# The low part of one weight slab in four, added up by a DMA from SBUF instead of VectorE's subtraction

## The reference

```python
def _even_mixer(h, w_in, a_conv, b_conv, b_conv_bias, b_ln_g, b_ln_b, w_out):
    p = h @ w_in                                   # (512, 2048) @ (2048, 7*1024)
    a_x, a_b, a_c, a_z, b_val, b_gate, b_z = jnp.split(p, 7, axis=-1)
    ya = a_b * _causal_dwconv(a_c * a_x, a_conv)   # 3 taps
    yb = b_val * jax.nn.sigmoid(b_gate)
    yb = _causal_dwconv(yb, b_conv) + b_conv_bias  # 31 taps
    yb = jax.nn.silu(_layernorm(yb, b_ln_g, b_ln_b))
    u = jnp.concatenate([ya * jax.nn.silu(a_z), yb * jax.nn.silu(b_z)], axis=-1)
    return u @ w_out
```

## Time and profile before

| | us |
|---|---|
| time, three runs | 1404.67 median (1404.5 to 1405.18) |
| span of the profiled execution | 1402.8 |
| PE busy | 1377.8 (98%) |
| DVE busy | 698.9 (50%) |
| ACT busy | 384.5 (27%) |
| POOL busy | 109.9 (8%) |
| mean traffic of the DMA engines | 110 GB/s |

### The profile page before, as it was taken

How to read it: one execution, slowest core, us unless ns; L and a number is a source line. 1 busy time by engine, 2 the same in 40 slices (tenths; PEclk the granted TensorE clock), 3 DMA queues, 4 the chain that set the end, 5 groups by cost and what they waited for, 6 DMA issues and landing times.

```text
span 1402.8 us, 16146 instructions
## 1 busy us (share of the span) xinstructions
PE 1377.8 (98%) x6466; PEld 1156.4 (82%) x6466; DVE 698.9 (50%) x767; ACT 384.5 (27%) x413; POOL 109.9 (8%) x101
## 2 busy tenths in 40 slices
PE   5999999999999999999999999999999999999997
PEld 4988888888888888888888899888888888888886
DVE  7588888888753223334332585444522222722333
ACT  5332233222222122223321353222222223512220
POOL 5100000000008200000000000000000003400000
PEclk9999999999999999999999999999999999999999
DMA  8243333434243333333422364333333322262204
GB/s 245 61 111 95 94 112 98 120 90 112 71 127 90 109 90 91 90 105 137 178 90 95 119 205 121 92 99 105 96 90 100 109 90 90 64 236 90 90 30 180
DMA packets 208307, 154.82 MB, mean 110 GB/s; under 512 B 2576, under 2 KB 187024, under 8 KB 205968
## 3 DMA queue, kind: packets, MB, share of 16 engines
q1 hardware_dynamic: 207120, 145.94, 35.1%
q10 hardware_dynamic: 1152, 8.39, 1.6%
HBM read 145.93 MB, written 8.39 MB: 110 GB/s over the span
## 4 chain that ended last, share of the span: by engine, by line
PE 96%; DVE 2%; issue 1%; DMA 0%; ACT 0%; DVEq 0%; POOLq 0%; POOL 0%
PE bank L417 32%; PE bank L418 32%; PE bank L419 32%; DVE h_lo L971 1%; DVE scratch L977 1%; PE bank L447 0%; DVE rows L964 0%; DMA rows<-x_t 0%; DVE diagonals L942 0%; DVE w_lo L986 0%; DVE rows L1128 0%; PE bank L476 0%; PE bank L485 0%; ACT scratch L682 0%; PE bank L545 0%
## 5 line engine op out<-in xcount | busy, mean ns | idle before, releaser
L417 PE MATMUL bank<-h_hi,w_hi 128*128 128x512 f32 (+1 forms) x1600 | 597.3, 373 | 4.9 <-DVE h_lo L971 4.8
L418 PE MATMUL bank<-h_lo,w_hi 128*128 128x512 f32 (+1 forms) x1600 | 595.3, 372 | 0.0
L419 PE MATMUL bank<-h_hi,w_lo 128*128 128x512 f32 (+1 forms) x1600 | 595.3, 372 | 0.0
L909 DVE TENSOR_TENSOR w_lo<-raw,w_hi 128x2048 fp32r<-128x2048 f32 x121 | 280.3, 2317 | 215.7 <-ACT w_hi L650 194.7
L417 PEld LDWEIGHTS bank<-h_hi,w_hi 128*128 128x128 f32 x1600 | 301.4, 188 | 59.3 <-issue 4.5
L419 PEld LDWEIGHTS bank<-h_hi,w_lo 128*128 128x128 f32 x1600 | 301.4, 188 | 52.6
L418 PEld LDWEIGHTS bank<-h_lo,w_hi 128*128 128x128 f32 x1600 | 301.4, 188 | 52.4 <-issue 0.5
L650 ACT ACTIVATE w_hi<-raw 128x2048 fp32r<-128x2048 f32 x122 | 233.3, 1912 | 238.2 <-PE bank L419 189.6
L1004 DVE SCALAR_TENSOR_TENSOR rows<-shifted,vecs,rows 128x512 f32 x256 | 198.0, 776 | 42.2 <-ACT rows L720 10.9
L417 PE MATMUL bank<-w_hi,h_hi 128*128 128x512 f32 x512 | 199.5, 390 | 0.0
L419 PE MATMUL bank<-w_hi,h_lo 128*128 128x512 f32 x512 | 199.3, 389 | 0.0
(11 more groups left out here) (79 smaller groups left out, 442.6 us busy)
## 6 DMA issues: line engine op xcount, KB each, us to landing
raw<-e_in SPq DMA_DIRECT2D x54, 1024.0 KB, 5.6
raw<-o_in SPq DMA_DIRECT2D x32, 1024.0 KB, 6.0
raw<-e_out SPq DMA_DIRECT2D x16, 1024.0 KB, 5.1
raw<-o_out SPq DMA_DIRECT2D x16, 1024.0 KB, 5.0
rows<-x_t SPq DMA_DIRECT2D x8, 512.0 KB, 6.5
x_mid<-rows ACTq DMA_DIRECT2D x4, 1024.0 KB, 4.8
raw<-o_cw SPq DMA_DIRECT2D x4, 1024.0 KB, 5.3
out<-rows SPq DMA_DIRECT2D x3, 1024.0 KB, 3.9
```

Source lines behind the costliest of these rows:

```text
L417: nc.tensor.matmul(dst, w[0], m[0], start=first, stop=False)
L418: nc.tensor.matmul(dst, w[0], m[1], start=False, stop=False)
L419: return nc.tensor.matmul(dst, w[1], m[0], start=False, stop=last)
L909: nc.vector.tensor_tensor(w_lo[:, slot, :], raw[:, slot % RAW, :], f32(w_hi[:, slot, :]), ALU.subtract)\
```

## The change

In each of the eight steps of the convolution stage, the low part of slab 4c + 4 (slot 0, raw buffer 0) is made differently. ScalarE, after the high part, writes the negative of the rounded slab into `w_lo` (the new `minus_hi`, one more activation of 128 by 2048). GpSimd then issues a DMA from `raw` to `w_lo`, both in SBUF, that adds to what is there. VectorE does no subtraction for this slab; after taps 1 to 10 it waits for the DMA and raises `lo_ready` by one. Lines of the changed kernel are 6 to 12 higher.

```diff
@@ gpsimd
             for c in range(CB):
+                pool.wait_ge(minus_hi_ready, c + 1)
+                nc.gpsimd.dma_start(w_lo[:, 0, :], raw[:, 0, :], accum_op=ALU.add)\
+                    .then_inc(lo_added, 16)
                 pool.wait_ge(conv_done, c + 1)
                 nc.gpsimd.tensor_tensor(csum, csum, tile(c + CB), ALU.add)\
                     .then_inc(csum_ready, 1)
@@ scalar
+            def minus_hi(slot):
+
+                nc.scalar.activation(w_lo[:, slot, :], raw[:, slot % RAW, :], ACT.Copy,
+                                     scale=-1.0).then_inc(minus_hi_ready, 1)
+
...
                 nc.scalar.activation(sig, bank[0][:, :], ACT.Sigmoid).then_inc(bank_free[0], 1)
                 split_ahead(c, 1)
+                minus_hi(0)
                 act.wait_ge(bank_free[1], c + 2)
@@ vector
                 chain[1] = c * links
-                split_ahead(c, 1)
                 dve.wait_ge(slab_done, done(c * SLOTS + 2))
...
                 convolve(c, conv_done, glu, CONV_B, "conv_b", 1, 11)
+                dve.wait_ge(lo_added, c * 16 + 16)
+                dve.sem_inc(lo_ready, 1)
                 split_ahead(c, 2)
```

## The result

| | us | ratio to before, 95% interval |
|---|---|---|
| before, 4 runs | 1404.93 (1404.5 to 1405.73) | |
| changed, 4 runs | 1410.40 (1410.25 to 1411.63) | 1.0041 (1.0025 to 1.0057) |
| span, profiled execution | 1402.8 before, 1408.4 changed | |

A forecast was written before the change was run, and what follows sets the result against it. The prediction took TensorE to bound the kernel, with VectorE close behind. A 3.9 us stall and 2.0 us of low clock, added to 1404.67, gave 1410.6 us, range 1408.0 to 1417.0.

The forecast's parts named there:

- The bound: Convolution stage: TensorE is busy for all 348.36 us; other engines' work costs or gains only through TensorE's waits.
- The subtraction that goes: VectorE, eight of 2.29 us, 18.3 us in all; TensorE waited for none, so removing them gives nothing by itself.
- The count that moves: `lo_ready` raised behind ten taps makes TensorE wait 3.9 us for slab 4, once, at the head of step 1.
- What hangs on the count: SyncE's load of slab 4c + 6, later splits and ScalarE's extra 15.2 us: no cost.
- The DMA: Step 0: 8.3 us including issue, hidden behind ten taps in up to 9.85 us, with 1.5 us to spare.
- such a stop: VectorE holding up GpSimd's issue of the DMA: 1.5 us more, 9.8 in all; two stops, 11.3, exceed the cover.
- The clock: After the stall at step 1, TensorE's clock likely falls to half for 4.0 us, losing 2.0 us.
- Rival 1: The 3.9 us stall at step 1 comes but the clock holds: 1408.6 us; chance 0.24.
- The sum: 3.9 us of stall plus 2.0 us of clock, 5.9 us, added to 1404.67: 1410.6 us; chance 0.38.
- a late DMA: DMA exceeds 9.85 us; VectorE, then TensorE, wait, each us over costing one, once: 1414.2 at 13.4 us; chance 0.31.
- a DMA of 20 us: Costs in every step: 3.9 + 10.15 in step 0, 3.3 in seven more, 37 us, plus clock: about 1443.

The follow-up runs named there:

- The count alone: Kernel before, with VectorE's subtraction kept, no copy or DMA, only the raise of `lo_ready` moved behind ten taps: 1411.62 us against 1404.79.
- the earlier tap 0: Changed kernel with ScalarE's negative copy moved behind its tap 0: 1407.94 us against 1404.79 for the kernel before.
- the run with two DMAs: Changed kernel with GpSimd's adding DMA issued twice, the second when the first has landed: 1416.64 us against 1405.37 for the kernel before.
- the plain copy: Changed kernel with the adding DMA replaced by a non-adding one of the same megabyte from `w_hi` to `w_lo`: 1411.92 us against 1405.03, one execution each.
- nine taps: Changed kernel with the wait for the DMA and the raise of `lo_ready` behind tap 9, tap 10 following: 1409.40 us against 1405.37 for the kernel before.

## Why the prediction was right

- **The bound.** Right. Outside the stall and the low clock behind it the kernel takes the same time (1326.6 us from step 1 on where the clock held, 1326.4 before), though VectorE lost 20 us of work.
- **The subtraction that goes.** Nothing by itself, as priced.
- **The count that moves.** Right, step by step: tap 1 at 71.04 for 71.3, taps ended at 79.88 for 80.15, wait 3.86 for 3.9. That whole execution ran 0.2 us ahead of the one predicted from (the last matmul of step 0 started at 76.05 for 76.25), so the difference is nearly nil. The count alone gave 5.3, the earlier tap 0 gave 2.1.
- **What hangs on the count.** No cost, as priced. ScalarE idled 12.9 us for the later load, and the split behind tap 20 still began at 91.29 for 91.3.
- **The DMA.** Hidden, as forecast. The size was too high: in step 0 it was 7.5 us from the end of the copy (70.06 to 77.6) for 8.3. An adding DMA takes 1.6 times the plain one here, 7.0 us to 4.5, and not twice. The rule of the Trainium skill, "Collectives: The Full Stack", section "The bandwidth ceiling: the fold count and why AG ≠ RS ≠ AR", that an adding transfer costs double, is too strict here for the whole DMA: 7.0 against 4.5. The estimate from the Trainium skill, "DMA: Bandwidth & Descriptors", section "Anatomy of one DMA — SWDGE (gpsimd) path", 6.8 us for twice a megabyte, is near the measured 7.0. No run shows an effect of VectorE on issuing. The issues took 0.87 to 1.06 us in all eight, the longest the first, which began with VectorE idle; in the run with two DMAs the second issue of step 0, at 78.36, took 0.87 us in the midst of VectorE's taps (72.52 to 80.44). The rule of the shared port, from the Trainium skill, "SBUF — State Buffer", section "Who interferes with whom", is not seen at work on an issue in these rows. The 1.5 us that the prediction gave such a stop came from two different additions, 1.67 us for line 380 and 3.21 for line 392. Line 392 has a median of 1.29 us in the trace of before, so that one was held up by 1.9.
- **The clock.** It fell, as forecast; the term was 2.0 us and the profile of the changed kernel has 1.7 to 1.8, that of the plain copy 2.6 behind the same wait. The ground, that 3.9 us is longer than the 2.7 after which it fell in the earlier trace rows, pointed the right way: it held in the profiles with waits of 1.4 and 2.1 us and was low in those with 3.0, 3.9, 5.3 and 8.6. But 2.7 us is no fixed delay: from the end of the last matmul to the fall the profiles have 2.1 us (plain copy) to 5.1 (count alone). That the size came out so near is in part luck. It was taken from the earlier trace rows, where matmuls took twice as long from 18.30 on, for 4.0 us; the profile gives a granted clock of 1.00 over that whole stretch, so the low level there rests on the lengths of the rows alone, and nothing tied the length of that stretch to the one behind a stall, which was 3.4 us here and 6.8 and 10.2 in others. Rival 1, the wait without the clock's loss, came in three of eight executions behind a pause of 3.0 us. The mean granted clock of the changed kernel, 0.998 in the profiled execution, where it fell, and 0.997 in the three others, speaks for a fall in all four.
- **The sum.** 1410.6 for 1410.4, or 5.9 us over before for 5.5. The term of the clock was 0.2 or 0.3 us too large against the profiled execution, which is within what runs differ by; the median of before moved by 0.26 us between the two measurements, which brought the two times nearer than the two losses are. The prediction gave this outcome 0.38 and a late DMA 0.31. That the DMA would be hidden was a guess between 3.9 and 13.4 us, and it held with 2.3 us to spare. For a DMA of 20 us the prediction's own terms (1404.67 + 37.1 + 2.0) give about 1444, not 1443.

## What to carry to other kernels

When a count stands in order with other work on a queue, its place is a cost of its own: price it at the tightest consumer, which was here the first turn of the loop, before the steady state had built its margin. Moving work off an engine that nobody waits for gained nothing here, and the semaphore that replaced it lost what the work never cost. A pause of TensorE may have to be charged with its clock as well: it held in the profiles behind 1.4 and 2.1 us, fell in five executions of eight behind 3.0, and cost 1.7 to 2.6 us behind 3.9.

## What the runs showed of the hardware

An adding DMA of 1 MB from SBUF to SBUF, issued by GpSimd, took 7.0 us from the start of its issue to landing (6.9 to 7.4 over eight) and a plain one 4.5, with 0.88 and 0.57 us of GpSimd's time. The clock can fall after TensorE has resumed: in the changed kernel at about 80.5, with work again from 80.19, and with nine taps at about 80.3, with work from 79.36. It can also fall in the pause: at 79.0 with the plain copy, with work again from 80.68. The low stretch was 3.4 us in the profiles of the changed kernel, the count alone and nine taps, 6.8 us with the plain copy and 10.2 us with two DMAs. What is lost is half of the part in which TensorE works: 1.7 us of the 3.4, 2.6 of the 6.8 (5.1 us with work), 2.5 of the 10.2 (4.9 us with work). Thirty-two matmuls of 128 columns in the pause of the changed kernel (3.7 us of them) kept the granted clock at 1.00.
